# A mixture of experts taken four experts at a time, in 32-row strips, with unrounded products

## The reference, cut to what matters

```
g_sel = argmax(g_logits + b_group)                    # 1 of 4 groups
_, top_idx = top_k(e_logits + e_bias, 2)              # 2 of the group's 8 experts
gate = one_hot(g_sel) * local_w * g_w                 # 32 gates, two of them not zero
a = einsum('sd,edf->sef', h, w_gate)                  # d = 1024, f = 256, e = 32
u = einsum('sd,edf->sef', h, w_up)
x = x + einsum('sef,efd->sd', silu(a) * u * gate, w_down)
```

## Time and profile before

| | before |
|---|---|
| median of 3 runs | 930.98 us (929.9 to 931.35) |
| span of the profiled execution | 929.2 us |
| TensorE busy | 919.7 us, 99% |
| VectorE, ScalarE busy | 739.5 and 623.4 us |
| bytes read and written | 217.13 MB, mean 234 GB/s |

### The profile page before, as it was taken

One profiled execution on the slowest core, in us unless ns is written; L12 is line 12 of the kernel. 1 busy time (PEld: TensorE's weight loads), 2 busy tenths in 40 slices (PEclk: granted clock), 3 DMA queues, 4 the chain that ended last, 5 costly groups with the idle time before them and its releaser, 6 DMA issues.

```text
span 929.2 us, 13554 instructions
## 1 busy us (share of the span) xinstructions
PE 919.7 (99%) x5004; PEld 797.4 (86%) x5004; DVE 739.5 (80%) x1110; ACT 623.4 (67%) x948; POOL 26.9 (3%) x47
## 2 busy tenths in 40 slices
PE   9999999999999999999999999999999999999997
PEld 7888888888888888888888899999998888888886
DVE  6657686668999999999999889888896655555576
ACT  5785686676777877878878765847575544434456
POOL 2500000000000000000010000000000000000000
PEclk9999999999999999999999999999999999999999
DMA  9755426523699999999999364837456665555531
GB/s 338 250 180 177 164 77 245 179 90 137 232 353 359 368 399 385 364 401 372 362 363 392 117 204 148 264 117 230 158 198 232 200 206 182 181 183 180 190 125 46
DMA packets 103519, 217.13 MB, mean 234 GB/s; under 512 B 5773, under 2 KB 60593, under 8 KB 97841
## 3 DMA queue, kind: packets, MB, share of 16 engines
q1 hardware_dynamic: 101072, 211.70, 64.8%
q0 software_dynamic: 2096, 4.64, 1.7%
q10 hardware_dynamic: 304, 0.20, 0.1%
HBM read 213.89 MB, written 2.63 MB: 233 GB/s over the span
## 4 chain that ended last, share of the span: by engine, by line
PE 93%; DVE 4%; ACT 1%; issue 1%; DMA 0%; DVEq 0%; ACTq 0%
PE bank L2398 21%; PE bank L2400 21%; PE bank L2399 21%; PE bank L3217 5%; PE bank L3218 5%; PE bank L3219 5%; PE bank L2415 4%; PE bank L2411 3%; PE bank L2405 2%; PE bank L2406 2%; PE bank L2752 1%; DVE w_lo L470 1%; DMA silu_g<-in_mem_norm_g_dram 0%; DVE w_lo L468 0%; PE bank L2478 0%
## 5 line engine op out<-in xcount | busy, mean ns | idle before, releaser
L2398 PE MATMUL bank<-w_hi,xT_hi 128*128 128x512 f32 (+2 forms) x626 | 247.6, 396 | 0.4 <-DVE w_lo L464 0.3
L2400 PE MATMUL bank<-w_hi,xT_lo 128*128 128x512 f32 (+2 forms) x626 | 243.1, 388 | 0.0
L2399 PE MATMUL bank<-w_lo,xT_hi 128*128 128x512 f32 (+2 forms) x626 | 242.6, 388 | 0.0
L2400 PEld LDWEIGHTS bank<-w_hi,xT_lo 128*128 128x128 f32 x626 | 117.8, 188 | 24.2
L2398 PEld LDWEIGHTS bank<-w_hi,xT_hi 128*128 128x128 f32 x626 | 118.5, 189 | 22.8 <-issue 0.5
L2399 PEld LDWEIGHTS bank<-w_lo,xT_hi 128*128 128x128 f32 x626 | 118.1, 189 | 22.1
L468 DVE TENSOR_TENSOR w_lo<-stage,w_hi 128x1024 fp32r<-128x1024 f32 (+3 forms) x94 | 107.4, 1142 | 25.9 <-ACT w_hi L454 24.3
L3217 PE MATMUL bank<-hT_hi,w_hi 128*128 128x256 f32 x440 | 123.3, 280 | 0.1
L3218 PE MATMUL bank<-hT_lo,w_hi 128*128 128x256 f32 x440 | 123.1, 280 | 0.0
L3219 PE MATMUL bank<-hT_hi,w_lo 128*128 128x256 f32 x440 | 123.1, 280 | 0.0
L454 ACT ACTIVATE w_hi<-stage 128x1024 fp32r<-128x1024 f32 (+3 forms) x96 | 95.6, 995 | 28.6 <-PE bank L2400 13.3
(11 more groups left out here) (493 smaller groups left out, 1509.6 us busy)
## 6 DMA issues: line engine op xcount, KB each, us to landing
stage<-in_w_in_dram SPq DMA_DIRECT2D x36, 1024.0 KB, 5.3
stage<-in_w_gate_up_dram SPq DMA_DIRECT2D x44, 512.0 KB, 4.8
stage<-in_expert_w_gate_dram SPq DMA_DIRECT2D x33, 512.0 KB, 6.1
stage<-in_expert_w_up_dram SPq DMA_DIRECT2D x33, 512.0 KB, 6.9
second<-in_expert_w_down_dram SPq DMA_DIRECT2D x16, 1024.0 KB, 7.1
stage<-in_expert_w_down_dram SPq DMA_DIRECT2D x15, 1024.0 KB, 7.3
stage<-in_w_down_dram SPq DMA_DIRECT2D x11, 1024.0 KB, 4.8
stage<-in_w_out_dram SPq DMA_DIRECT2D x8, 1024.0 KB, 5.1
```

What stands on the lines that cost most here:

```text
L2398: mm(o, k_hi, v_hi, start=start, stop=False)
L2399: mm(o, k_hi, v_lo, start=False, stop=False)
L2400: return mm(o, k_lo, v_hi, start=False, stop=stop)
```

## The change

The 128 slots now belong to four experts, 32 to each: expert j of a quad has output rows 32j to 32j+31 (`strip(j)`), so eight quads replace four groups of eight turns. Each strip's products are single, unrounded float32 `mm` on the weight as it was loaded, with 32 stationary columns in place of 128. Expert units are never rounded or split; they are loaded whole into 17 places (`places`: memory of `w_hi`, `w_lo`, `stage`, `xs` and of tensors of the attention that are dead by then) and one more, `rows_unit`, used once; units 0 to 17, a quad and a half, are issued before the stage. `gather` takes `x` unrounded, in a view with a stride of 8 values. Every quad returns its rows at once on TensorE, with the sum over quads in banks 0 to 3, so POOL's writes and fetches are gone. The routing decides over all 32 experts by fields of 2 x 5 x 8 cells. The embedding's products become single ones and stand behind quad 6. If an expert has more than 32 tokens, a loop over all 32 experts follows.

```diff
-        def columns_of(half, u0, g, j):
-            pe.wait_ge(st.lo_ready, g * PER_TURN + (u0 + 1))
-            s, o = u0 % RING, expert_columns(st, g, j)[:, :]
-            for k in range(4):
-                kk = 4 * half + k
-                ins = three(o, xg_hi[:, kk], xg_lo[:, kk], w_hi[:, s, 512 * k:512 * k + 512],
-                                w_lo[:, s, 512 * k:512 * k + 512], start=kk == 0, stop=kk == KD - 1)
-            ins.then_inc(st.unit_done, 1)
+        x_blocks = x[:].rearrange("p t (q k) -> p t k q", k=KD)
+        def gather(q):
+            pe.wait_ge(sem("slots_filled"), q + 1)
+            for k in range(KD):
+                for t in range(T):
+                    ins = mm(bank[4 + k // 4][:, P * (k % 4):P * (k % 4) + P], x_blocks[:, t, k], slot_of[:, t], start=t == 0, stop=t == T - 1)
+                if k % 4 == 3:
+                    ins.then_inc(sem("expert_gathered"), 1)
+        def columns(q, kind):
+            units = [QUAD_UNITS * q + QUAD * kind + j for j in range(QUAD)]
+            units_here(pe, q, kind)
+            for k in range(KD):
+                if kind == 0 and k % 4 == 0:
+                    pe.wait_ge(sem("rows_ready"), 2 * q + k // 4 + 1)
+                for j, i in enumerate(units):
+                    ins = mm(bank[6][strip(j), FF * kind:FF * kind + FF], xg[:, k, strip(j)], expert_unit(i)[:, FF * k:FF * k + FF],
+                             start=k == 0, stop=k == KD - 1)
+        def down(q):
+            units_here(pe, q, 2)
+            pe.wait_ge(sem("hidden_copied"), q + 1)
+            pe.wait_ge(sem("rows_ready"), 2 * min(q + 2, QUADS))
+            for c in range(2):
+                for k in range(2):
+                    at = D * k + 512 * c
+                    for j, i in enumerate(units):
+                        ins = mm(bank[4 + c][strip(j), :], hiddenT[:, k, strip(j)], expert_unit(i)[:, at:at + 512], start=k == 0, stop=k == 1)
+        gather(0)
+        for q in range(QUADS):
+            columns(q, 0)
+            turn_slots(q)
+            columns(q, 1)
+            if q < QUADS - 1:
+                gather(q + 1)
+            turn_hidden(q)
...
+            down(q)
+            bring_back(q)
+            if q == QUADS - 2:
+                for t in range(T):
+                    embed_products(t)
...
+        def gather_scaled(q):
+            for n in range(2):
+                dve.wait_ge(sem("expert_gathered"), 2 * q + n + 1)
+                ks = slice(4 * n, 4 * n + 4)
+                tt(xg[:, ks], bank[4 + n][:, :].rearrange("p (k s) -> p k s", k=4), gather_g[:, ks].unsqueeze(2).to_broadcast([P, 4, P]), ALU.mult)\
+                    .then_inc(sem("rows_ready"), 1)
...
+        for u, units in ((U_CO + 1, (16, 17)), (U_CO + 2, (0, 1)), (U_CO + 3, (2, 3, ROWS_UNIT))):
+            sp.wait_ge(unit_done, u + 1)
+            for i in units:
+                load_expert(sp, i)
+        for i in range(LAPS + 1, QUADS * QUAD_UNITS):
+            unit_read(sp, before_in_place(i))
+            load_expert(sp, i)
...
+        sp.wait_ge(sem("downs_done"), 2 * QUAD * (QUADS - 1))
```

More of the change, by code:

```diff
@@ L285, in program @@
[L285 to L288, removed]
+    over_keys, over_values, over_scores = (eb(n, [P, SLOT])[:] for n in ("over_keys", "over_values", "over_scores"))
+    raw_turned = eb("raw_turned", [P, KD, T * P])
+    over_latent = [eb(f"over_latent{n}", [P, SLOT])[:] for n in range(2)]
+    logits, biased, diffs, exps = (eb(n, [P, T, FIELDS * PER_GROUP]) for n in ("logits", "biased", "diffs", "exps"))
@@ L365, in program, with __init__ @@
     class Stream:
[L366 to L372, removed]
+        def __init__(self, places, pairs):
+            self.places, self.pairs, self.halved = places, pairs, (0, 1)
+            self.landed = [sem(f"weights_landed{s}") for s in range(RING)]
+            self.up_landed = [sem(f"up_landed{s}") for s in range(RING)]
+            self.hi_ready, self.lo_ready = sem("w_hi_ready"), sem("w_lo_ready")
+            self.half_ready, self.unit_done = sem("w_half_ready"), sem("unit_done")
@@ L374, in slot @@
         def slot(self, u):
-            p = self.places[u]
-            return stage[:, p] if p < RING else more[p - RING][:]
+            return stage[:, self.places[u]]
         def uses(self, u, pairs_only=False):
-            known = self.earlier.uses_of(self.places[u], pairs_only) if self.earlier else 0
-            return known + sum(self.places[v] == self.places[u] and (not pairs_only or v in self.pairs or v in self.halved) for v in range(u + 1))
-        def uses_of(self, place, pairs_only):
-            return sum(p == place and (not pairs_only or v in self.pairs or v in self.halved) for v, p in enumerate(self.places))
+            return sum(self.places[v] == self.places[u] and (not pairs_only or v in self.pairs or v in self.halved) for v in range(u + 1))
@@ new lines, in experts_of, with flat_of, across, by_token @@
+        def experts_of(v):
+            return by_group(v)[:, :, 0:GROUPS]
+        def flat_of(v):
+            return v[:].rearrange("p t n -> p (t n)")
+        def across(v):
+            return v.unsqueeze(2).to_broadcast([P, rows, PER_GROUP])
+        def by_token(v):
+            return v.rearrange("p (t o) -> p t o", t=T)
+        equal, hot1, weights, hot1_mine = (field(n) for n in range(4))
+        best, best_logit, best_mine = small(0), small(1), small(2, T)
+        group_sum, expert_sum, group_weight = small(3, T), small(4, T), small(5, T)
@@ new lines, in add_returned @@
+        def add_returned(returned, signal):
+            for n in range(4):
+                dve.wait_ge(sem(returned), n + 1)
+                dst = x[:, n % 2, 512 * (n // 2):512 * (n // 2) + 512]
+                tt(dst, dst, bank[n][:, :], ALU.add).then_inc(sem(signal), 1)
+        for q in range(QUADS):
+            if q == QUADS - 1:
+                over_flag = overflow(dve)
+            expert_quad(q)
+        add_returned("expert_returned", "x_moe")
+        with dve.If(over_flag < 1):
+            split_lo(dve, SLOT, U_HEADS)
@@ new lines, in turn_slots @@
+        def turn_slots(q):
+            if q == 0:
+                pe.wait_ge(sem("token_gates"), 2)
+                been_read(pe, "rank")
+            for j in range(QUAD):
+                for t in range(T):
+                    mm(bank[7][strip(j), 0:2], slot_of[:, t, strip(j)], token_gates[:, t, QUAD * q + j], start=t == 0, stop=t == T - 1)
+            for t in range(T):
+                ins = transpose(bank[7][:, 2 * P + P * t:2 * P + P * t + P], slot_of[:, t])
+            ins.then_inc(sem("slots_turned"), 1)
@@ L3116, in _ @@
+        with pe.If(over_flag > 0):
             overflow_experts()
```

1035 lines of the change are left out of this document (324 added, 711 removed), and 2 rows, old and new, of the table products.

## The result

The changed kernel takes 867.23 us (median of four runs, 863.09 to 869.16) against 931.06 for the kernel before on the same chip: a ratio of 0.931, interval 0.9285 to 0.9337, so 64 us are gone where 25 were forecast. The profiled execution took 863.09 us, its span is 861.2.

A forecast was written before the change was run, and what follows sets the result against it. TensorE was taken as the bound, transfers close behind. At 30.4 us a quad, the stage takes 246.0 us, from 244.2 to 490.2; with 2.1 at the end, 25.2 us are saved: 905.8, rounded to 905, range 866 to 930.

The forecast's parts named there:

- rival 1: Expert stage: strips overlap fully and transfers become the bound; 19.5 us of TensorE a quad, 878 us (865 to 893), chance 0.28.
- the two limits close together: Expert stage before the change: TensorE busy 272.6 of 273 us, DMA queues in use 98% at 366 GB/s; TensorE sets the pace.
- the price of an unrounded product: Each unrounded float32 product leaves two records of 216 ns, 432 ns for 256 columns.
- the return of 2.2 us: End of each quad: copy and remainder of the second half plus two of the returning products' pairs, 2.2 us.
- the hand-over: Before a quad's down products: turning the hidden values, VectorE's scaling of the next rows and a signal, 1.2 us together.
- I take half: Gate, up and down products: strips overlap by half, 20.7 us a quad, between 41.5 without overlap and 10.4 with all four.
- TensorE's own sum ends at 490.2, so it stays the later one: Expert stage: TensorE ends at 490.2, transfers with down and return at 483.7, unless the rate falls under 356 GB/s.
- Loading ahead is therefore not what shortens the stage: Expert stage: fewer streamed columns, not units loaded early, were to shorten it, as TensorE ends after the transfers.
- The gather: Collecting the next quad's rows with every eighth value of x: 32 records, 3.5 to 6.9 us, taken as 5.2.
- The rate: The stage's 78 remaining units, 81.8 MB: 223.5 us at 366 GB/s, 196.2 at 417.
- The start: Routing ends at 237.0, first gather adds 5.2 and a lower clock 2.0: stage starts at 244.2, 4 us later than before.
- The end: Between the return and the head's first product, 2.5 us before: two units behind ScalarE's copy add 2.1 us.

The follow-up runs named there:

- the one-strip kernel: Changed kernel with all gate, up and down products of a quad writing output partitions 0 to 31, one expert after the other: 1089.9 us, 1.170 of the kernel before.
- The strip-by-strip kernel: Changed kernel with gate and up products ordered expert by expert, all eight k blocks each, instead of alternating strips for each k: 965.2 us, 1.036 of the kernel before.

## Why the prediction was wrong

What came true is rival 1, to which I had given 0.28. Right in the forecast were the two limits close together, the price of an unrounded product (two records, 216 ns apiece; the one-strip kernel shows it again), the return of 2.2 us (263.91 to 266.1), and the hand-over (1.2; it was 1.0). Two slips changed little: the slices between 353 and 401 GB/s are eleven, not twelve, and the last quad, which has no gather to hide it, waits 1.7 us for VectorE's work on the hidden values, which the sum left out.

**The step that failed is "I take half".** Its reason, that "records start in program order in every timeline" and that "the next product's first record can run beside the second, but not before it", was an observation of a kernel with one output at a time, where order and dependence can't be told apart. The strip-by-strip kernel shows records out of program order across strips, and the one-strip kernel the factor: 3.48 against 13.8 us, fourfold. In the sum, gate, up and down are 3.5 to 3.6 each in place of 6.9, 10.1 us less a quad; the gather takes 2.6 of it back, and the slots' gates need 0.6 in place of 1.1. The Trainium skill, "TensorE: Matmul & The Clock Gate", Part 3, which I had weighed with its 2.38 and 3.07 times, pointed the right way, and this trace has more, 4.0 with four column strips. Behind this step fell "TensorE's own sum ends at 490.2, so it stays the later one" and "Loading ahead is therefore not what shortens the stage": with TensorE at 22 us a quad it is worth 24 us.

**Mis-sized in the sum:**
- The gather: I took 5.2 of 3.5 to 6.9; it is 7.8, as one record takes 241 to 245 ns in place of 109. The bound from ScalarE's and VectorE's reads, one more cycle a value, was too low. The Trainium skill, "SBUF — State Buffer", on cachelines, speaks of a penalty for such steps, and the trace agrees with its sign. For the end it hardly mattered.
- The rate: 424 GB/s where I had 366 and 417 as ends. From the first free place (247.7) to the last transfer (445.3) 81.8 MB make 414 on the mean: the first bytes move about 1 us after the place is free, and from 441 us on the queue also carries the second block's pieces of 1 KB. The first rival's sum had 392 on the mean, and that is why its 878 was too high: its stage ended at 462.1, in truth at 451.2. The Trainium skill, "DMA: Bandwidth & Descriptors", Specifications, has 435 GB/s as the ceiling of the transfers into a core's memory; the trace agrees with 424. I had read 417 in one stretch of before as an upper end, where it was the lower bound of a limit not yet reached.
- The start: the gather began at 236.05, not 237.0 (the choice took less), and the columns at 243.89, as forecast (244.2), by luck: a gather dearer by 2.6 us cancels the 2.0 for the clock that were not lost and the 0.95 from the choice. The granted clock stood at 0.50 from 235.5 to 242 us, but the first gather took 7.84 us and the next, at 1.00, 7.72: the spacing of the values paces it at either level.
- The end: 3.9 us from the return to the head's first product, in place of 2.5; 1.4 more, where I had 2.1.

Together: the stage starts where I had it, ends 39.0 us earlier (451.2 for 490.2), and the tail is 0.7 shorter. The other 3.1 of the span's 42.8 us (861.2 for 904.0) lie behind the head's first product, where executions differ by that much; this profiled one is also the fastest of its four.

## What to carry to other kernels

Narrow products belong on different column strips in turn, product by product; one strip's worth at a time in the program loses most of the overlap. When TensorE becomes several times faster, price the stage by the bytes at the queue's full rate first, and ask when the first place comes free and whether the queue ever runs dry; from then on bytes, their piece size and that moment counted for over 20 us here, and each change of TensorE's order or work for 5 at most, so long as the strips took turns. An order seen where nothing could overlap is no evidence for what happens when something can.

## What the runs showed of the hardware

- Four column strips of float32 products run at 4.0 times one strip (3.48 and 13.8 us for 64 records), and TensorE sends about two products (four records) past a busy strip; records of different strips then start out of program order.
- A stationary block of 128x128 float32 values that lie 32 bytes apart costs 241 to 245 ns a record, at the granted clock of 0.5 as well as at 1.0 (7.84 and 7.72 us for 32); plain, 214 at 0.5 and 112 at 1.0.
- One queue of 1 MB loads in pieces of 8 KB holds 424 GB/s; in pieces of 2 KB it moves 409, in pieces of 1 KB 348 to 350; with two thirds of the bytes in pieces of 1 KB, 380 to 387.
- While TensorE waits for transfers the granted clock falls (0.59 on the mean from 370 to 380 us, with TensorE busy 4 of 10 us); in the last down products it was 0.51 in one of the changed kernel's two profiles and 1.00 in the other.
